# A one-core decoder layer with routed experts: embedding products, weight splits and the first gather placed elsewhere around the router

## What is computed

```
h  = x + concat(conv_branch, gated_mlp_branch) @ w_out          # w_out: 1024 x 1024
c  = rms_norm(h)
gl = c @ w_router_group + b ; el = c @ w_router_expert + b      # 4 and 16 logits
g  = argmax(gl) ; top 2 of the 4 experts of group g, with their weights
y  = sum over the two picked experts e: w_e * (silu(c @ w_gate[e]) * (c @ w_up[e])) @ w_down[e]
h  = h + y
h  = h + (p @ w_ple_proj) * sigmoid(rms_norm(h) @ w_ple_gate)   # p: 256 inputs per token
out = rms_norm(h)
```

## Time and profile before

| | us |
|---|---|
| median of 3 runs | 700.38 (699.4 to 700.95) |
| the profiled execution, its own time | 703.07 |
| its span from first to last instruction | 701.3 |
| PE busy | 619.7 (88%) |
| DVE busy | 517.4 (74%) |
| ACT busy | 356.5 (51%) |
| POOL busy | 194.9 (28%) |

### The profile page before, as it was taken

One profiled execution on the slowest core, in us unless ns is written; L12 is line 12 of the kernel. 1 busy time (PEld: TensorE's weight loads), 2 busy tenths in 40 slices (PEclk: granted clock), 3 DMA queues, 4 the chain that ended last, 5 costly groups with the idle time before them and its releaser, 6 DMA issues.

```text
span 701.3 us, 10279 instructions
## 1 busy us (share of the span) xinstructions
PE 619.7 (88%) x3672; PEld 545.3 (78%) x3672; DVE 517.4 (74%) x568; ACT 356.5 (51%) x359; POOL 194.9 (28%) x190
## 2 busy tenths in 40 slices
PE   3899999963899978779999999999999999539994
PEld 3799999833799977568888888888888888339994
DVE  5558997997312258468999999999999999487445
ACT  6611322311521261457777777777777777424233
POOL 7035646930020000461222222222222211111004
PEclk9999999955799986889999999999999999859997
DMA  9973120234110141469999999999999999470003
GB/s 279 337 213 121 61 93 29 68 120 169 42 61 31 61 130 32 156 156 378 396 393 391 384 389 361 392 370 368 388 382 357 389 380 356 143 269 1 1 1 136
DMA packets 75659, 154.02 MB, mean 220 GB/s; under 512 B 8331, under 2 KB 25315, under 8 KB 75043
## 3 DMA queue, kind: packets, MB, share of 16 engines
q1 hardware_dynamic: 68075, 138.45, 55.4%
q0 software_dynamic: 5664, 10.08, 4.1%
q10 hardware_dynamic: 1888, 5.05, 2.1%
HBM read 147.90 MB, written 14.41 MB: 231 GB/s over the span
## 4 chain that ended last, share of the span: by engine, by line
PE 76%; DVE 10%; DMA 3%; POOL 3%; issue 3%; ACT 3%; SPq 1%; POOLq 0%; ACTq 0%; DVEq 0%
PE pair L1480 21%; PE pair L1482 20%; PE pair L1481 20%; PE pair L1532 8%; PE pair L1491 3%; DVE pair L1109 2%; DMA two<-in_state_conv 2%; POOL h L625 1%; PE pair L1747 1%; DVE lo L1065 1%; ACT act_hi L752 1%; POOL h L627 1%; PE pair L1654 1%; DMA raw<-pairs 1%; PE pair L1715 1%
## 5 line engine op out<-in xcount | busy, mean ns | idle before, releaser
L1480 PE MATMUL pair<-hi,act_hi 128*128 128x512 f32 (+2 forms) x828 | 291.7, 352 | 13.6 <-DVE lo L1065 4.0
L1482 PE MATMUL pair<-hi,act_lo 128*128 128x512 f32 (+2 forms) x828 | 284.9, 344 | 0.0
L1481 PE MATMUL pair<-lo,act_hi 128*128 128x512 f32 (+2 forms) x828 | 284.7, 344 | 0.0
L1065 DVE TENSOR_TENSOR lo<-raw,hi 128x2048 fp32r<-128x2048 f32 x110 | 249.0, 2290 | 35.4 <-ACT hi L752 35.2
L752 ACT ACTIVATE hi<-raw 128x2048 fp32r<-128x2048 f32 x119 | 225.0, 1917 | 82.3 <-PE pair L1482 44.8
L1480 PEld LDWEIGHTS pair<-hi,act_hi 128*128 128x128 f32 (+1 forms) x828 | 156.5, 189 | 36.6 <-issue 8.6
L1482 PEld LDWEIGHTS pair<-hi,act_lo 128*128 128x128 f32 (+1 forms) x828 | 155.9, 188 | 18.5
L1481 PEld LDWEIGHTS pair<-lo,act_hi 128*128 128x128 f32 (+1 forms) x828 | 156.7, 189 | 16.4
L1109 DVE SCALAR_TENSOR_TENSOR pair<-conv,vecs,pair 128x512 f32<-128x512 f32 x112 | 74.8, 747 | 0.0
L676 POOL DMA_INDIRECT pairs<-two,sidx x17 | 43.0, 2528 | 111.6 <-DVE two L1347 111.6
L752 ACT ACTIVATE act_hi<-pair 128x1024 fp32r<-128x1024 f32 (+3 forms) x49 | 38.4, 795 | 54.7 <-PE pair L1491 35.0
(11 more groups left out here) (194 smaller groups left out, 547.4 us busy)
## 6 DMA issues: line engine op xcount, KB each, us to landing
raw<-in_w_exp_gate SPq DMA_DIRECT2D x34, 1024.0 KB, 9.8
raw<-in_w_exp_up SPq DMA_DIRECT2D x34, 1024.0 KB, 9.0
raw<-in_w_exp_down SPq DMA_DIRECT2D x34, 1024.0 KB, 10.2
raw<-in_w_in SPq DMA_DIRECT2D x8, 1024.0 KB, 11.6
h<-in_x_prompt SPq DMA_DIRECT2D x8, 512.0 KB, 6.8
raw<-in_w_out SPq DMA_DIRECT2D x4, 1024.0 KB
raw<-in_w_ple_gate SPq DMA_DIRECT2D x4, 1024.0 KB, 9.8
raw<-pairs SPq DMA_DIRECT2D x4, 1024.0 KB, 8.0
```

Of the source, the lines that this page charges most:

```text
L1065: nc.vector.tensor_tensor(lo[:, n % SPLIT, :], raw[:, n % RAW, :], hi[:, n % SPLIT, :].bitcast(F32), ALU.subtract).then_inc(lo_dve, 1)
L1480: mm(out_, x_hi, w_hi, start=start, stop=False)
L1481: mm(out_, x_hi, w_lo, start=False, stop=False)
L1482: return mm(out_, x_lo, w_hi, start=False, stop=stop)
```

## The change

- ACT, in the last round of the loop over tiles: the splits of units 12 and 13 come ahead of `router_input(3)`; in every round `router_input(t - 1)` comes ahead of the squares of tile t instead of behind them. Before, the two splits stood behind the copies to `phi`.
- DVE: `split_low` of unit 12 comes after the addition of quarter 2 of tile 4, instead of after `plo`. That of unit 13 stays.
- PE: `router_rows(t - 1)` comes after quarter 2 of tile t instead of after quarter 3, and `router_logits(3)` ahead of the transposes of the embedding's inputs.
- PE: `embedding(2)` comes between the ranks and the ten pairs of list products, instead of behind these.
- PE: `transpose_gathered(0)` no longer waits for ACT's copies of the embedding; that wait comes behind it.
- POOL: the first gather takes its row numbers from `lists` itself; the copy to `gidx` and the wait for it are gone for this one, and the count that the others wait for is one lower.

```diff
@@ -663,7 +663,7 @@
                     g.wait_ge(gathered, 16 * (e0 + d))
                     g.wait_ge(g_ps, e0 + d)
                 nc.gpsimd.tensor_copy(gidx[:, :], lists[:, bass.ds(e0 + d, 1), 0]).then_inc(gidx_set, 1)
-                wait_all(g, (gidx_set, e0 + 2 + d))
+                wait_all(g, (gidx_set, e0 + 1 + d))
                 nc.gpsimd.indirect_dma_start(xg, None, normed, bass.IndirectOffsetOnAxis(gidx[:, :], 0),
                                              bounds_check=last_token, oob_is_err=False).then_inc(gathered, 16)
 
@@ -683,7 +683,8 @@
 
             g.wait_ge(lists_in, 1)
             g.wait_ge(gidx_set, 1)
-            gather(0)
+            nc.gpsimd.indirect_dma_start(xg, None, normed, bass.IndirectOffsetOnAxis(lists[:, 0, 0:1], 0),
+                                         bounds_check=last_token, oob_is_err=False).then_inc(gathered, 16)
             gather(1)
             g.wait_ge(slots_clear, 16)
             g.wait_ge(slot_at, 1)
@@ -894,20 +895,21 @@
 
             act.wait_ge(store, 16 * (3 + DEC_BATCH))
             for t in range(TILES):
+                if t == TILES - 1:
+                    split_high(N_PROJ)
+                    split_high(N_MOE)
+                if t >= 1:
+                    router_input(t - 1)
                 act.wait_ge(o_add, OUT_ORDER.index((D // UC - 1, t)) + 1)
                 act.wait_ge(sq_done, TILES + t)
                 square(t, FFN)
                 root(FFN, t)
-                if t >= 1:
-                    router_input(t - 1)
             for t in range(TILES):
                 act.wait_ge(pt_ps, min(2 * (t // 2) + 2, TILES))
                 copy(phi[:, :, t * P:t * P + rows(t)],
                      pt_out(t).rearrange("p (c n) -> p c n", c=2)[:, :, 0:rows(t)]).then_inc(pt_hi, 1)
-            split_high(12)
-            split_high(13)
             router_input(TILES - 1)
-            split_high(14)
+            split_high(N_MOE + 1)
             load_gain("norm_ple_g")
             for i in range(2):
                 act.wait_ge(arg_done, i + 1)
@@ -1228,13 +1230,14 @@
                 nc.vector.tensor_tensor(at, bank[3 + q % 3][0:rows(t), 0:UC], at, ALU.add).then_inc(o_add, 1)
                 if i == 1 and t >= 1:
                     ffn_norm(t - 1)
+                if (i, t) == (D // UC - 2, TILES - 1):
+                    split_low(N_PROJ)
             ffn_norm(TILES - 1)
             for t in range(TILES):
                 v.wait_ge(pt_hi, min(2 * (t // 2) + 2, TILES))
                 nc.vector.tensor_tensor(plo[:, :, t * P:t * P + rows(t)],
                                         pt_out(t).rearrange("p (c n) -> p c n", c=2)[:, :, 0:rows(t)],
                                         phi[:, :, t * P:t * P + rows(t)].bitcast(F32), ALU.subtract).then_inc(pt_lo, 1)
-            split_low(N_PROJ)
             split_low(N_MOE)
 
             v.wait_ge(small_in, 16 * 4)
@@ -1668,11 +1671,12 @@
                 token_rows(t, n, bank[3 + q % 3], o_ps)
                 if i == 1 and t >= 2:
                     router_logits(t - 2)
-                if i == D // UC - 1 and t >= 1:
+                if i == D // UC - 2 and t >= 1:
                     if t == 1:
                         pe.wait_ge(state_sb, 2)
                     router_rows(t - 1)
 
+            router_logits(TILES - 2)
             pe.wait_ge(p_in, 16 * TILES)
             pe.wait_ge(o_add, TILES * D // UC)
             for t in range(TILES):
@@ -1680,7 +1684,6 @@
                 for c in range(2):
                     ins = tr(pt_out(t)[:, c * P:c * P + r], PN[0:r, t, c * P:(c + 1) * P], ident[0:r, 0:r])
                 ins.then_inc(pt_ps, 1)
-            router_logits(TILES - 2)
             router_rows(TILES - 1)
             router_logits(TILES - 1)
             pe.wait_ge(pt_lo, TILES)
@@ -1709,13 +1712,14 @@
             mm(bank[5][:, 0:TILES * EXPERTS], before[:, :], M.rearrange(flat), start=True, stop=False)
             mm(bank[5][:, 0:TILES * EXPERTS], ones[:, :], earlier.rearrange(flat), start=False, stop=True)
             mm(bank[5][:, P:P + EXPERTS], ones[:, :], r16[:, 5, 0, :], start=True, stop=True).then_inc(rank_ps, 1)
+            embedding(2)
             for k in range(2):
                 for t in range(TILES):
                     pe.wait_ge(picked, TILES * k + t + 1)
                     ins = mm(bank[4][:, 0:2 * EXPERTS], pick[k][0:rows(t), t, :], load[0:rows(t), k, t, :],
                              start=(k == 0 and t == 0), stop=(k == 1 and t == TILES - 1))
             ins.then_inc(list_ps, 1)
-            for t in range(2, TILES):
+            for t in range(3, TILES):
                 embedding(t)
 
 
@@ -1773,8 +1777,8 @@
                 transpose_hidden(e0, d)
 
             pe.wait_ge(lg_sb, 1)
+            transpose_gathered(0)
             pe.wait_ge(pp_sb, TILES)
-            transpose_gathered(0)
             step(0)
             step(1)
             with pe.Fori(0, STEPS - 3) as d:
```

## The result

The changed kernel takes 688.91 us (median of 4, 688.79 to 689.77) against 700.08 (median of 4, 699.4 to 700.95): ratio 0.9834, 95% interval 0.9807 to 0.986. In three later jobs the ratio was 0.9848 (0.9818 to 0.9878), 0.9872 (0.9848 to 0.9896) and 0.9834 (0.9811 to 0.9857); the medians of the four jobs differ by 11.2, 11.3, 8.3 and 10.6 us.

The account below looks back on a forecast made before the run. PE was taken to bound the kernel, so starting the expert steps earlier ends it earlier: expert 0 10.7 us sooner, less allowances 0.9 and 1.9, gives 7.9, so 700.4 - 7.9 = 692.5 us; range 689.7 to 697.0 (about 0.8).

Parts of the forecast that it names:

- The router's chain: DVE's start on the router after tile 4's logits and unit 13's split: 258.3 instead of 260.69 us, gain 2.4.
- The list product: PE's 20 records after `embedding(2)`: 2.4 us at full clock, bounds 2.4 and 4.9, ending at 271.1 instead of 275.17.
- The first gather: POOL's transfer issued 0.3 us after the lists, landing at 276.3, just before PE is free; decides 0.3 or so.
- the two allowances: Taken off the 10.7 us gain: 0.9 for some work at the lower clock, 1.9 for the profiled execution's bad luck.
- I take most of it, 1.9, as its bad luck: Kernel before, list product to about the end of `embedding(2)`: low clock cost the profiled execution 2.3 us, 1.9 deducted.
- I take a third, 0.9: Part of the 36 steps and 20 records at the lower clock in a given run: 2.6 us, a third deducted.
- step 0 and step 1 keep their shape: Expert steps behind the stretch: the events they hang on move along, so they change nothing.
- the clock stays low in the middle: Rival, chance 0.18: `embedding(2)` and list product at the lower clock, expert 0 at 287.5, gain 3.3, say 697 us.
- only the router's chain moves: Rival, chance 0.05: ACT or the gather ends last and PE's gain is waiting; 2.4 us, 698.0.
- the gather's slow bound: Rival, chance 0.05: first gather issued 1.1 us after the lists, landing 0.5 us after PE is free; 693.
- slower: Rival, chance 0.04: `embedding(2)` blocks the list product, lower clock throughout; expert 0 2.3 us later, 702.7.
- no change: Rival, chance 0.02: a later transfer holds step 1 at its old time.

Follow-up runs that it names:

- a_gather_copy: Changed kernel with the first gather through `gidx` again, copy and wait before it; 691.12 us, ratio 0.9863 to the kernel before.
- front_only: Kernel before with only the edits of ACT, DVE, `router_rows` and `router_logits(3)`; 699.94 us, ratio 0.9962.
- a_no_embed: Changed kernel with `embedding(2)` back behind the list product; 697.01 us, ratio 0.9926 to the kernel before.
- b_filler: Kernel before with 12 products that nobody reads added between ranks and list product, nothing moved; 700.61 us, ratio 0.9984.
- before_fourth: Kernel before, no edit, a fourth profiled execution; 701.91 us (one run).
- before_again: Kernel before, no edit, profiled again; 703.22 us, ratio 1.0007.
- c_low17_low13: c_low17 with DVE's split of unit 13 moved behind the lists and eight small operations moved later; 689.56 us, ratio 0.9839 to the kernel before.
- c_all: c_low17_low13 with `embedding(2)` and (4) cut into halves, the first gather's transposes between the halves of (4); 686.72 us, ratio 0.9800 to the kernel before.
- c_low17_halves: c_low17 with c_all's halves of `embedding(2)` and (4), without moving unit 13's split and the job list; 690.24 us, ratio 0.9835 to the kernel before.
- b_embed: Kernel before with only `embedding(2)` moved between the ranks and the list product; 697.58 us, ratio 0.9936.
- a_late_transposes: Changed kernel with the wait for ACT's copies again ahead of the first gather's transposes; 693.08 us, ratio 0.9894 to the kernel before.
- c_low17: Changed kernel with DVE's split of unit 17 moved ahead of the hidden product of step 0; 688.99 us, ratio 0.9822 to the kernel before.

## Why the prediction was wrong

The steps up to expert 0 held; what was put on top of them did not, and one step behind it was not as forecast. Shifted by the 2.1 us that the first mark came earlier, the forecast's events and the measured ones:

| event | forecast | measured |
|---|---|---|
| last addition to h | 248.9 | 248.90 |
| router's chain starts | 256.2 | 255.98 |
| embedding(0) starts | 255.9 | 254.88 |
| embedding(2) ends | 266.6 | 266.4 |
| list product ends | 269.0 | 269.1 |
| first gather issued, behind the end of the lists | 0.3 | 0.3 |
| gather seen by SP, behind its issue | 4.6 | 4.5 |
| transposes start | 274.5 | 274.61 |
| first product of expert 0 | 278.0 | 278.09 |

**The router's chain** came 2.6 us sooner, forecast 2.4. One term was mis-sized, with little effect: the logits of tile 4 took 1.08 us and not 1.87, because the row that I took (16 records in 1.87 us) stood at the lower clock (0.50 over this row) and they now ran at the upper (1.00). Where they ran at the lower clock again, in a_gather_copy, the chain started 0.3 us later. Half as many weight columns as in the 128-row tiles, 1.86 us each at full clock, would have told it. PE then waited 0.64 us for the one-hot matrix.

**The list product** at 2.6 us (forecast 2.4, with a bound of 4.9) was the largest single item, and the mechanism named for it is shown: 2.6 us in all ten traces of the seven kernels with a whole embedding or its like right ahead, 4.5 to 4.9 in all six of the three without (before, front_only, a_no_embed), and fast when useless work was put there (b_filler). The Trainium skill, "TensorE: Matmul & The Clock Gate", the section on the HAM clock gate, says that the monitor runs freely of the kernel; the traces bear it out for the places where the clock falls and rises (the first half of the list product took 2.07 to 2.45 us in the four traces of before, and the clock rose behind it about three us sooner in before_fourth), but the list product took 4.5 to 4.9 us in all four of before and 2.6 in all four of the changed kernel, not now one and now the other.

**The first gather** was forecast as a near tie with PE, "0.3 or so"; without the edit PE waits 0.60 us and the stretch between lists and transposes is 0.8 longer. The size was low, the sum untouched.

**The failed step** is the two allowances: "I take most of it, 1.9, as its bad luck" and "I take a third, 0.9". The sum of the stretch was 10.7 and 10.6 was measured; the allowances took 2.8 from it. The profiled execution of before was indeed 2.7 us above its median, and I gave that to the one place where I could imagine it. The repeats put it elsewhere: the stretch is 43.4 in three traces of four, 41.76 in one, while the time up to the first mark goes from 244.96 to 248.25 us over all kernels, with and without the change. The span of before_again is 1.8 us shorter than that of the first trace: 2.25 less up to the first mark, 0.05 in the stretch, 0.5 more behind it. The second allowance was for a fall of the clock behind the list product that none of four traces of the changed kernel has, and three of its variants have (c_low17_low13, c_all, c_low17_halves). Without the two the forecast would have been 700.4 - 10.7 = 689.7, with 688.91 to 691.91 measured in four jobs.

**A term put at nothing** is the other failed step: "step 0 and step 1 keep their shape". From expert 0 to expert 3 the four traces of the changed kernel are 1.1 to 1.4 us shorter than the four of before. Against three of these the difference is all in step 1, where the clock comes back sooner behind PE's wait of 4.0 us; against before_fourth it is in step 0, which has the clock down for longer. With it the marks of the first traces give 93.33 - 81.48 = 11.9 us. Why it comes back sooner stays open. Of the variants that keep the old place of the split of unit 17 only a_no_embed has it too (48.8 us from expert 0; front_only, b_embed, b_filler, a_late_transposes and a_gather_copy have 49.7 to 50.2), so it isn't shown to belong to the change.

The medians of the kernel before differ by 2.5 us between jobs (700.08 to 702.61) and the gain in the medians goes from 8.3 to 11.3, so the time alone doesn't tell 10.6 from 11.9.

The rivals: that the clock stays low in the middle did not come; that only the router's chain moves is refuted by front_only (0.9962 against 0.9834); the gather's slow bound (1.1 us behind the lists) fell, 0.3; slower and no change are refuted.

## What to carry to other kernels

Small products behind an idle TensorE can cost twice what they need: look at the granted clock over them, and put dense work that is due anyway right ahead of them, even if it delays them a little. When a sum of steps, each from a row, is complete, the difference between the profiled time and the median belongs to no step until a second trace shows where it is; take it out of the range, not out of the forecast. An order that frees PE exposes what hid behind it: the copy and the gather's issue cost something only then. And a gain has to be followed past the place where it arises: c_low17's 2.3 us at expert 1 were gone at expert 3, in a wait that was not there before.

## What the runs showed of the hardware

The 16 records of the logits with 128 weight columns took 1.86 us at the upper clock, with 64 columns 1.08, and 1.87 at the lower: with the same 20 columns streamed, their pace changed with the weight columns and with the clock. The first indirect transfer of 128 rows of 4 KB, with DMA share 0.00 ahead of it, was seen by its waiter 4.3 to 4.9 us after its start on POOL; the third one of c_low17, beside loads of weights, 10.4 us after it (297.98 to 308.42). The time up to the first mark differed by 3.1 us between executions of the changed kernel; what sets that was not looked for.
